# A one-hot gate matrix: its rows scaled by GpSimd between gathers instead of by ScalarE, in a ring of four buffers

## The reference, cut to what matters

```
q = (xi @ w_pq).reshape(P_BLOCK, P_HEADS, 2, P_HALF)
s = jnp.einsum('thpd,hpkd->thpk', q, sub_keys)
sv, si = lax.top_k(s, P_TOPK)
...
g = jax.nn.softmax(fv, axis=-1)
act = jax.nn.gelu(jnp.einsum('thkd,td->thk', expert_u[eidx], xi), approximate=False)
return jnp.einsum('thk,thkd->td', (g * act), expert_v[eidx])
```

## Time and profile before

| | |
|---|---|
| median of three runs | 4818.48 us (4811.77 to 4832.81) |
| profiled execution, its own time | 4828.28 us |
| its span | 4826.4 us |
| PE, DVE, ACT, POOL busy | 77%, 63%, 19%, 37% of the span |
| DMA | 1227 MB, mean 254 GB/s |

### The profile page before, as it was taken

How to read it: one execution, slowest core, us unless ns; L and a number is a source line. 1 busy time by engine, 2 the same in 40 slices (tenths; PEclk the granted TensorE clock), 3 DMA queues, 4 the chain that set the end, 5 groups by cost and what they waited for, 6 DMA issues and landing times.

```text
span 4826.4 us, 37323 instructions
## 1 busy us (share of the span) xinstructions
PE 3739.4 (77%) x11392; PEld 2151.2 (45%) x11392; DVE 3061.8 (63%) x5972; ACT 915.4 (19%) x1737; POOL 1798.6 (37%) x1567
## 2 busy tenths in 40 slices
PE   7767786895697874786663876556999899898997
PEld 2434554553453443443342544554444444444453
DVE  1132203111687888797777888777888888888821
ACT  1141001101220332112222213773000001100000
POOL 0000000000565556575332224334666666666600
PEclk9865696897798555897565987557999999999998
DMA  6101221234999788899554777778999999999952
GB/s 249 66 18 65 79 74 36 74 100 153 329 355 342 254 290 309 318 405 346 180 168 151 251 241 237 229 217 306 409 409 408 408 399 409 403 403 399 406 190 88
DMA packets 434556, 1227.29 MB, mean 254 GB/s; under 512 B 39740, under 2 KB 160700, under 8 KB 430276
## 3 DMA queue, kind: packets, MB, share of 16 engines
q0 software_dynamic: 221184, 805.40, 44.9%
q1 hardware_dynamic: 106176, 209.81, 12.3%
q10 hardware_dynamic: 107024, 210.04, 11.8%
HBM read 1158.71 MB, written 66.39 MB: 254 GB/s over the span
## 4 chain that ended last, share of the span: by engine, by line
DVE 21%; PE 21%; DMA 14%; issue 10%; POOL 8%; ACT 1%; SPq 0%; ACTq 0%; DVEq 0%
DMA expert_rows<-in_expert_u,expert_index 10%; POOL expert_rows L2742 8%; PE ps_all L2151 4%; DVE expert_rows L2943 3%; DVE acc L2959 3%; PE ps_all L2472 2%; PE ps_all L2463 2%; PE ps_all L2452 2%; PE ps_all L1594 2%; DVE keep L2428 2%; PE ps_all L1582 1%; PE ps_all L1789 1%; PE ps_all L2174 1%; PE ps_all L1819 1%; PE ps_all L1792 1%
## 5 line engine op out<-in xcount | busy, mean ns | idle before, releaser
L2742 POOL DMA_INDIRECT expert_rows<-in_expert_v,expert_index x768 | 902.1, 1175 | 950.0 <-DVE acc L2959 416.0
L2742 POOL DMA_INDIRECT expert_rows<-in_expert_u,expert_index x768 | 886.3, 1154 | 681.5 <-DVE acc L2959 296.1
L2943 DVE CUSTOM_DVE_ANT_0 expert_rows<-expert_rows,h_rows_sb 128x1024 f32<-128x1024 f32 x768 | 921.7, 1222 | 160.4 <-DMA expert_rows<-in_expert_u,expert_index 147.4
L2959 DVE SCALAR_TENSOR_TENSOR acc<-expert_rows,weights,acc 128x1024 f32<-128x1024 f32 x756 | 937.0, 1289 | 23.2 <-DMA expert_rows<-in_expert_v,expert_index 20.3
L2472 PE MATMUL ps_all<-branchT,side 128*128 128x512 f32 x1536 | 705.8, 610 | 76.9 <-DVE side L2437 72.0
L2463 PE MATMUL ps_all<-hT,branchT 128*128 128x384 f32 x2048 | 694.3, 493 | 45.7 <-ACT side L2411 29.5
L2463 PEld LDWEIGHTS ps_all<-hT,branchT 128*128 128x128 f32 x2048 | 393.8, 193 | 354.3 <-issue 121.5
L2472 PEld LDWEIGHTS ps_all<-branchT,side 128*128 128x128 f32 x1536 | 298.0, 196 | 442.2 <-issue 323.5
L2151 PE MATMUL ps_all<-hT,side 128*128 128x384 f32 x1152 | 393.3, 499 | 39.2 <-ACT hT L2232 20.9
L2151 PEld LDWEIGHTS ps_all<-hT,side 128*128 128x128 f32 x1152 | 222.8, 195 | 197.9 <-ACT hT L2232 21.5
L2452 PE MATMUL ps_all<-keep 128*128 128x128 f32 x768 | 174.7, 415 | 142.1 <-issue 70.3
(11 more groups left out here) (399 smaller groups left out, 4562.9 us busy)
## 6 DMA issues: line engine op xcount, KB each, us to landing
branchT<-in_expert_uT ACTq DMA_DIRECT2D x128, 512.0 KB, 6.9
branchT<-in_expert_vj ACTq DMA_DIRECT2D x128, 512.0 KB, 9.2
w_mod_ring<-in_w_mod SPq DMA_DIRECT2D x12, 2048.0 KB, 9.8
gate_rows<-branchT ACTq DMA_DIRECT2D x12, 2048.0 KB, 11.6
keep<-gate_rows ACTq DMA_DIRECT2D x32, 768.0 KB, 11.7
side<-in_w_blk SPq DMA_DIRECT2D x40, 512.0 KB, 6.8
expert_rows<-in_expert_u,expert_index POOLq DMA_INDIRECT x768, 11.0
expert_rows<-in_expert_v,expert_index POOLq DMA_INDIRECT x768, 10.0
```

The source lines that it names most:

```text
L2742: pool.indirect_dma_start(rows[:, r % ROWS, :], None, io[table], bass.IndirectOffsetOnAxis(ap=eidx[:, q % 3, k:k + 1], axis=0)).then_inc(r ...
L2943: dve.tensor_tensor_reduce(rows[:, r % ROWS, :], rows[:, r % ROWS, :], h2[:, :], 1.0, 0.0, ALU.mult, ALU.add, dot[:, j, k:k + 1]).then_inc ...
L2959: dve.scalar_tensor_tensor(own, rows[:, r % ROWS, :], wgt[:, j, k:k + 1], own, ALU.mult, ALU.add).then_inc(row_used, 1)
```

## The change

The loop on ScalarE that scales the one-hot rows of i is gone. In its place GpSimd does one multiply of 128x512 for each group (`pool_gates`), with the gate broadcast along the row. GpSimd's instructions are in one queue with its gathers: a table `due` puts each multiply ahead of the gather that is issued 12 rows after the row operation behind which VectorE makes the group. TensorE waits for one signal per group instead of four. The ring of one-hot tiles has four buffers instead of three. The beat of a pair of groups has other numbers in the planner (3.8 and 2.6 in place of 5.2 and 2.8), and so the groups and the experts behind them go to other halves.

```
-        self.one = over.rearrange("p (s c t i) -> p s c t i", s=3, c=2, t=4)
+        self.one = [keep[:, at:at + 1024].rearrange("p (c t i) -> p c t i", c=2, t=4) for at in (0, 1024, 2048, G + 9 * P)]
...
     def scalar_gates(self, act, pair):
         groups = (2 * pair, 2 * pair + 1)
-        for b in groups:
-            d, t = divmod(4 * b, P)
-            act.wait_ge(self.one_ready, b + 1)
-            for n in range(4):
-                own = self.one[:, b % 3, 0, n, :]
-                act.activation(own, own, ACT.Copy, scale=self.dT[:, d, 2, t + n:t + n + 1]).then_inc(self.one_scaled, 1)
...
-            if b >= 3:
-                dve.wait_ge(self.g_psum, b - 2)
-            dve.tensor_tensor(self.one[:, b % 3], self.dT[:, d, 0:2, t:t + 4].unsqueeze(3).to_broadcast([P, 2, 4, PK]),
+            if b >= 4:
+                dve.wait_ge(self.g_psum, b - 3)
+            dve.tensor_tensor(self.one[b % 4], self.dT[:, d, 0:2, t:t + 4].unsqueeze(3).to_broadcast([P, 2, 4, PK]),
                               self.iota[:, :, :].unsqueeze(2).to_broadcast([P, 2, 4, PK]), ALU.is_equal).then_inc(self.one_ready, 1)
             yield
+
+    def pool_gates(self, pool, b):
+        d, t = divmod(4 * b, P)
+        own = self.one[b % 4][:, 0]
+        pool.wait_ge(self.one_ready, b + 1)
+        pool.tensor_tensor(own, own, self.dT[:, d, 2, t:t + 4].unsqueeze(2).to_broadcast([P, 4, PK]), ALU.mult).then_inc(self.one_scaled, 1)
...
-            pe.wait_ge(self.one_scaled, 4 * b + 4)
+            pe.wait_ge(self.one_scaled, b + 1)
...
-    beats += [("turned", 0, 3, 0, 0)] + [("gates", b, 5.2, 2.8, 2) for b in range(Dense.GROUPS // 2)]
+    beats += [("turned", 0, 3, 0, 0)] + [("gates", b, 3.8, 2.6, 2) for b in range(Dense.GROUPS // 2)]
...
+            due = {}
+            for n, half in enumerate(halves[:-1]):
+                first = u_row(n // 2 + 1) if n % 2 == 0 else v_row(n // 2)
+                total, at = sum(steps for _, _, steps in half), 0
+                for kind, b, steps in half:
+                    for e in range(steps):
+                        k = min(x for x in range(K) if (x + 1) * total // K > at)
+                        at += 1
+                        if kind == "gates":
+                            due.setdefault(first + k + ROWS, []).append(2 * b + e)
+
             def gather(q, table, first):
                 for k in range(K):
                     r = first + k
+                    for b in due.pop(r, ()):
+                        dense.pool_gates(pool, b)
```

More of the change, by code:

```diff
@@ L2451, in tensor @@
             for n in range(4):
-                mm = pe.matmul(ps[:, b % 4, n * PK:(n + 1) * PK], self.one[:, b % 3, 0, n, :], self.one[:, b % 3, 1, n, :],
+                mm = pe.matmul(ps[:, b % 4, n * PK:(n + 1) * PK], self.one[b % 4][:, 0, n, :], self.one[b % 4][:, 1, n, :],
                                start=True, stop=True)
```

## The result

The changed kernel takes 4777.39 us, median of five runs (4772.32 to 4789.39), against 4818.48 before, here of five runs too (4811.77 to 4832.81). The ratio is 0.9918 with a 95% interval of 0.9895 to 0.9941; the medians differ by 41 us. The forecast was 4831, slightly slower and inside what can't be told from no change. The time lies in the stated range of 4715 to 4900, which is wide enough to hold a gain and a loss, but the kernel moved the other way.

A forecast was written before the change was run, and what follows sets the result against it. ScalarE's scaling loop paces the gate stage and DMA the next; after the change GpSimd and VectorE take turns. Gate stage -3, DMA stage +67, tail -51.5 sum to +12 us on the median 4818.5: 4831, range 4715 to 4900.

The forecast's parts named there:

- Turns: Gate stage: GpSimd's multiply and VectorE's two-SBUF-input instructions each wait for the other's whole instruction; chance 0.45 at 2.3 to 2.75 us per group.
- The price of a turn: Gate stage: comparison 1.14, multiply 1.27 and 0.13 us give 2.54 us per group; stage 309 us, 3 us gained.
- handing over: Gate stage: 0.13 us per group, the time a gather spends ahead of its read, 0.94 - 0.81.
- a short hold: Rival, gate stage: GpSimd shuts VectorE out for only 0.61 us, 1.88 us per group, 63 us less: 4768; chance 0.12.
- the low end of the sum: Gate stage: with a multiply of 1.04 us the stage is 22 us shorter, 4809 us in all.
- The rest of the stage's order: Gate stage: 12 groups and about 14 row operations, one `choose` of 9.7 us, two halves of 42 groups and 16 row operations.
- The prediction's own sign of being wrong: Wrong altogether if the first expert comes before 3290, or the DMA stage does not grow by about 67 us.
- the case of the 0.30: Whole kernel faster by over 0.5%: short hold 0.12 and side by side 0.18 together.
- The transition: Last group out of PSUM to first expert's gate multiply: 28.5 us of stores and loads stay; forecast change 0.
- What moves: 40 row operations and five experts go to the full-DMA stage, 67 us more; five experts leave the tail, 51.5 us less.
- The ring closes: Rival, gate stage: GpSimd cannot get in between back-to-back comparisons; VectorE idles once per run, 69 us: 4900; chance 0.25.
- Side by side: Rival, gate stage: GpSimd's reads don't shut VectorE out, TensorE sets the pace; stage 198 us, 4719 in all; chance 0.18.

## Why the prediction was wrong

- **Turns: right.** The multiply and VectorE's instructions with two SBUF inputs take turns, as read from two gathers' waits. Comparisons last 2.05 us. That an instruction with one input holds no gather up was read from a weak row: the MATCH_REPLACE8 of the earlier trace rows lists two inputs, and it ends at 3357.48, 0.06 us after the gather's read would begin by the prediction's own 0.13. The gather of 0.98 us beside comparisons that read PSUM shows it properly. And "each waiting for the other's whole instruction" was half right: GpSimd waits for the whole of VectorE's, VectorE only for a part of GpSimd's.
- **The price of a turn: wrong, and this is the step that failed.** The sum had "1.14 + 1.27 + 0.13 = 2.54 us of the shared path" per group; it was 1.97. I took the middle between a copy's full time and that plus half a MEMSET, and added a handing over. The multiply's own time was the low one of these two, 1.035 us, and of it only the reading, 0.83 us, holds VectorE up. The other 0.20 us and the writing lie beside VectorE's next instruction, and there is no handing over. The difference, 0.57 us, is 55 us over 96 groups; with -3 it would have been -58, and -63 were measured. The other 5 us: VectorE's waits in the stage sum to 75 us by the means of its instructions, not to 96 x 0.83 = 80. With -63 the sum is -47 or -48 where it was +12, and with the +5 at the transition and 4 more where DMA is full it is the -38 measured. The pieces were in the rows: 0.84 ns an element in the copies times 1024 is 0.86. Of the rivals "a short hold" was near, with 1.88 us per group and 4768 us, though its 0.61 us came from the wrong place.
- **A stated bound that was none.** I called 1.04 us per multiply, plus the 0.13, the low end of the sum, 4809 us. The bound from below has to ask what part of an instruction uses what is shared. It can be much less than its duration.
- **The rest of the stage's order: right.** One `choose` in the stage and 46 row operations.
- **The prediction's own sign of being wrong came true.** The first expert comes at 3260.7 us, before 3290, and the stage has 249 us, not 309. The forecast's chances stood at 0.70 for the same or slower and 0.30 for over 0.5% faster, and the case of the 0.30 came.
- **The transition: +5 us, forecast 0.** Row operations run in it now, as forecast, but their gathers are then in flight as the first gate load is issued. From its issue to the first gate multiply it took 3260.70 - 3241.45 = 19.3 us, and 12.0 before (issued at 3319.25); waiting for the stores took less (9.1 us from the last store's issue to the first load's, 11.5 before). That gathers in flight are the cause was not tried. The issues, after and before:

```profile
3241.45 0.95 ACTq L2398 DMA_DIRECT2D keep<-gate_rows  x2
...
3319.25 0.95 ACTq L2404 DMA_DIRECT2D keep<-gate_rows  x2
```

- **What moves: right**, +71.2 for +67 and -51.6 for -51.5.
- **The ring closes: wrong**, with a chance of 0.25. In this kernel GpSimd does get in between two comparisons: three of them last 5.17 us, two of the three with a wait. One gather's wait of 2.00 us was read as a rule; the gate stage before has only one more like it (at 3155.19), and the same trace has a gather at 4593.80 that got in between two of six row operations without a gap:

```profile
4592.24 7.33 DVE L2959 SCALAR_TENSOR_TENSOR acc<-expert_rows,weights,acc 128x1024 f32<-128x1024 f32 x6
...
4593.80 1.73 POOL L2742 DMA_INDIRECT expert_rows<-in_expert_v,expert_index  x1 [5.35 <-DVE acc L2959]
```

  Why the two long ones waited for both comparisons stays open.
- **Side by side** is what the kernel would have done without VectorE's second SBUF input: forecast 198 us for the stage and 4719 us, measured 202.1 and 4722 with the indices in PSUM. That the numbers meet is partly luck: the forecast had TensorE set the pace and no waits, the run has VectorE at the pace with 29 us of waits in its row operations.

## What to carry to other kernels

Before moving elementwise work to GpSimd, count the SBUF inputs of VectorE's instructions beside it: with two, each element that GpSimd reads was paid again on VectorE here (0.83 ns for 128 rows); with one in PSUM, nothing was. Price a shared resource by the part of the instruction that uses it, not by its duration. And where a planner's numbers go with a change, cut the gain by stage: here GpSimd's multiplies with the old plan and the new plan with ScalarE were each worth nothing, together 0.8%.

## What the runs showed of the hardware

- GpSimd's elementwise instructions hold VectorE up by 0.40, 0.83 and 1.69 us for 512, 1024 and 2048 elements read per row, and its MEMSET of 512, which only writes, by nothing.
- A multiply of 128x512 on GpSimd takes 1.035 us alone, as long as its copy of 128x1024. The Trainium skill ("GPSIMD Engine Reference", section "Elementwise — side-by-side cycle accounting") gives 4497 ns for an add of 2048 columns; the multiply of 1024 took 1.89 us here, under half of that. This multiply works in place, with one input broadcast; whether that makes the difference was not tried.
- With VectorE full, a wait does not show as idle time of VectorE. It shows as longer instructions: 2.05 us for 1.21. A gather beside them shows 1.78 for 0.94.
- Profiled executions of programs with the same code ahead of 2963 us reached the first comparison at 2963 to 2991 us. A difference of that size in the span says nothing about the change; the stages behind it agreed to 5 us between profiles of kernels with the same plan.
